# Two half transfers for every weight chunk, and a limit on those under way in the expert stage

## What is computed

```
x = even_layer(...)        # mixer (mLSTM + differential attention), then a SwiGLU of width 2816
x = odd_layer(...)         # convolution mixer, then moe_swiglu
x = hybrid_layer(...) x 2  # three kinds of attention, gate, layer norm

def moe_swiglu(u, router_w, w1, w3, w2):       # 8 experts of width 2816, top 2
    logits = (tokens @ router_w)
    top_vals, top_idx = lax.top_k(logits, TOP_K)
    gates = jax.nn.softmax(top_vals, axis=-1)
    ...
    return (jax.nn.silu(xb @ w1[e]) * (xb @ w3[e])) @ w2[e]     # each block of tokens with its expert's weights
```

## Time and profile before

| | us |
|---|---|
| timed runs, median (lowest to highest) | 2010.14 (2007.98 to 2010.35) |
| the profiled execution: its own time | 2011.3 |
| the profiled execution: span from first to last instruction | 2009.5 |
| TensorE busy in the span | 1806.1 (90%) |
| weight loads (PEld) / VectorE / ScalarE busy | 1474.0 / 825.6 / 391.2 |
| moved by DMA | 480.22 MB, 239 GB/s on the mean |
| granted TensorE clock, mean | 0.945 |

### The profile page before, as it was taken

How to read it: one execution, slowest core, us unless ns; L and a number is a source line. 1 busy time by engine, 2 the same in 40 slices (tenths; PEclk the granted TensorE clock), 3 DMA queues, 4 the chain that set the end, 5 groups by cost and what they waited for, 6 DMA issues and landing times. The chain is left out here.

```text
span 2009.5 us, 43104 instructions
## 1 busy us (share of the span) xinstructions
PE 1806.1 (90%) x18202; PEld 1474.0 (73%) x18202; DVE 825.6 (41%) x2248; ACT 391.2 (19%) x1107; POOL 2.3 (0%) x6
## 2 busy tenths in 40 slices
PE   6999897999989887999988989978969998899987
PEld 4686666888868765789687887777658876688766
DVE  3756562778958812111110101011123766227651
ACT  3332333000014232000000000000021233112331
POOL 0000000000000000000000000000000000000000
PEclk8999998999999886999999999999989988899988
DMA  9622332899973222999999999999983412234100
GB/s 391 242 106 89 121 143 88 313 359 354 382 287 126 98 112 106 398 417 345 388 419 390 326 368 354 421 418 370 377 367 126 168 64 84 84 126 168 43 1 21
DMA packets 67909, 480.22 MB, mean 239 GB/s; under 512 B 7424, under 2 KB 9728, under 8 KB 9856
## 3 DMA queue, kind: packets, MB, share of 16 engines
q1 hardware_dynamic: 67712, 477.39, 60.7%
HBM read 476.32 MB, written 1.05 MB: 238 GB/s over the span
## 5 line engine op out<-in xcount | busy, mean ns | idle before, releaser
L518 PE MATMUL PS<-sb_U,sb_ring 128*128 128x256 f32 (+1 forms) x1456 | 376.5, 417 | 16.3 <-PEq L249 9.9
L518 PEld LDWEIGHTS PS<-sb_U,sb_ring 128*128 128x128 f32 x1456 | 284.3, 198 | 96.1 <-issue 59.6
L1710 PE MATMUL PS<-sb_arena,sb_ring 128*64 128x98 f32 (+3 forms) x5632 | 221.8, 239 | 38.4 <-issue 36.3
L1710 PEld LDWEIGHTS PS<-sb_arena,sb_ring 128*64 128x64 f32 x5632 | 214.6, 139 | 46.5 <-issue 43.6
L1738 PE MATMUL PS<-sb_ring,sb_arena 128*64 128x256 f32 x1344 | 158.4, 384 | 4.8 <-issue 4.2
L518 PE MATMUL PS<-sb_arena 128*64 128x128 f32 (+9 forms) x884 | 153.7, 350 | 7.2 <-DVE sb_arena L751 4.4
L789 PE MATMUL PS<-sb_U,sb_ring 128*128 128x256 f32 x704 | 155.5, 383 | 4.7 <-PEq L249 4.7
L789 PEld LDWEIGHTS PS<-sb_U,sb_ring 128*128 128x128 f32 x704 | 134.8, 192 | 25.3 <-issue 7.4
L518 PEld LDWEIGHTS PS<-sb_arena 64*128 64x128 f32 (+4 forms) x884 | 108.9, 176 | 46.0 <-issue 25.7
L374 DVE SCALAR_TENSOR_TENSOR sb_arena<-sb_ring,sb_cs,sb_arena 128x256 f32<-128x256 f32 x280 | 135.8, 485 | 10.0
L1738 PEld LDWEIGHTS PS<-sb_ring,sb_arena 128*64 128x64 f32 x1344 | 98.3, 137 | 51.5 <-issue 7.1
(11 more groups left out here) (344 smaller groups left out, 1622.6 us busy)
## 6 DMA issues: line engine op xcount, KB each, us to landing
sb_ring<-stream SPq DMA_DIRECT2D x446, 1024.0 KB, 8.2
sb_arena<-stream SPq DMA_DIRECT2D x4, 1024.0 KB, 7.9
sb_consts<-consts SPq DMA_DIRECT2D x1, 1773.5 KB, 26.3
sb_U<-ctxT SPq DMA_DIRECT2D x1, 1024.0 KB, 7.5
sb_XT<-xT SPq DMA_DIRECT2D x1, 1024.0 KB, 9.3
out<-sb_XT SPq DMA_DIRECT2D x8, 128.0 KB, 2.0
sb_small<-small SPq DMA_DIRECT2D x1, 292.0 KB, 2.7
sb_consts<-consts SPq DMA_DIRECT2D x1, 129.0 KB, 2.7
```

Source lines behind the costliest of these rows:

```text
L518: ins = pe.transpose(o, l, r) if t.turn else pe.matmul(o, l, r, start=s, stop=e)
L1710: ins = pe.matmul(PS[c:c + 64, m % 4, h * T:h * T + n], w[:, h, kt, c:c + 64], src[:, kt, 0:n], start=(kt == 0), stop=(kt == KT - 1))
```

## The change

Each chunk is now moved by two DMAs, one for rows 0 to 63 and one for rows 64 to 127, each with a semaphore of its own (26 in place of 13). Whoever waits for a chunk waits for both. This holds in all stages. In the expert stage SP waits, before it issues a half, until the half that is three before it in the stream has landed; so at most three halves (one and a half chunks) are under way.

```
+UNDER_WAY = 3
...
-    def landing(self, g):
-        return self.landed[self.turn(g) % RING] if self.home(g) is None else self.home_landed[self.home(g)]
+    def landing(self, g, part):
+        n = RING + self.home(g) if self.home(g) is not None else self.turn(g) % RING
+        return self.landed[2 * n + part]
 
     def wait(self, eng, g):
-        eng.wait_ge(self.landing(g), 16 if self.home(g) is not None else 16 * (self.turn(g) // RING + 1))
+        for part in range(2):
+            self.wait_part(eng, g, part)
+
+    def wait_part(self, eng, g, part):
+
+        eng.wait_ge(self.landing(g, part), 16 if self.home(g) is not None else 16 * (self.turn(g) // RING + 1))
+
+    def send(self, sp, g, source, under_way=None):
+
+        for part in range(2):
+            if under_way is not None:
+                self.wait_part(sp, *divmod(2 * g + part - under_way, 2))
+            rows = slice(part * (P // 2), (part + 1) * (P // 2))
+            sp.dma_start(self.chunk(g)[rows, :], source[rows, :]).then_inc(self.landing(g, part), 16)
...
-            sp.dma_start(self.chunk(g), self.dram[self.base + g]).then_inc(self.landing(g), 16)
+            self.send(sp, g, self.dram[self.base + g])
...
                 for g in range(MOD_FIRST):
-                    sp.dma_start(ws.chunk(g), ws.dram[g]).then_inc(landed[g % RING], 16)
+                    ws.send(sp, g, ws.dram[g])
...
-                    sp.dma_start(ws.chunk(g), source).then_inc(ws.landing(g), 16)
+                    ws.send(sp, g, source, UNDER_WAY)
```

More of the change, by code:

```diff
@@ L167, with __init__ @@
 class Stream:
-    def __init__(self, nc, ring, dram, sems, homes, home_sems, home_first):
+    def __init__(self, nc, ring, dram, sems, homes, home_first):
         self.nc, self.ring, self.dram, self.landed = nc, ring, dram, sems
-        self.homes, self.home_landed, self.home_first = homes, home_sems, home_first
+        self.homes, self.home_first = homes, home_first
         self.used = self.issued = 0
@@ L228, in clear @@
     def clear(self):
-        clear_together(self.nc, self.landed + self.home_landed)
+        clear_together(self.nc, self.landed)
 class Stage:
@@ L342, in area @@
             return arena[:, at:at + n]
-        landed = [ctx.enter_context(nc.semaphore(f"landed{i}")) for i in range(RING)]
-        home_landed = [ctx.enter_context(nc.semaphore(f"home_landed{i}")) for i in range(len(HOMES))]
-        ws = Stream(nc, ring, a["stream"], landed, [area(at, CH) for at in HOMES], home_landed, PRE_CH - OUT_CH + RING)
+        landed = [ctx.enter_context(nc.semaphore(f"landed{i}")) for i in range(2 * (RING + len(HOMES)))]
+        ws = Stream(nc, ring, a["stream"], landed, [area(at, CH) for at in HOMES], PRE_CH - OUT_CH + RING)
         late = ctx.enter_context(nc.semaphore("late_inputs"))
```

## The result

The changed kernel takes 2658.35 us (median of 4 runs, 2653.46 to 2668.7) against 2010.24 for the kernel before: a ratio of 1.322, 95% interval 1.319 to 1.326. The prediction was 2029 with a range of 1983 to 2075. The sign was right, but by luck: the two terms that gave it make 19 us of the 648 us measured, a factor of 34, and the cause named was the wrong one.

The account below looks back on a forecast made before the run. The prediction took the expert stage's weight DMA as the bound, with TensorE's instruction stops behind its shortfall; 11 us of stream plus 8 us of barrier on 2011.3, less 1.2, gave 2029 us, range 1983 to 2075.

Parts of the forecast that it names:

- the two terms that gave it: Expert stage: weight stream 11 us longer and 8 us more at the barrier, together 19 us.
- Halves in all stages: All stages: extra issues and waits taken as 0, range to 13 us; halves themselves 0, at most 0.33 us a chunk.
- the ports rival: Weight transfers: each half reaches only half of the SBUF's ports, a chunk takes 4.98 us, total about 2800 us; chance 0.10.
- The limit's stream term: Expert stage: under the limit the weight stream takes 727 us in place of 716.5, 11 us longer.
- The window just covers the latency: Expert stage: a half's turn takes 3.65 to 3.7 us, three halves fill the engines for 3.74 us, no slack.
- window too short: Expert stage: a turn takes 3.9 to 4 us and all packets cost 1.07 us, 46 us more, 2075; chance 0.07.
- 80 us for the instruction packets: Expert stage: 75 of 94 instruction packets each cost the weight stream 1.07 us, 80 us in all.
- The stops for instructions: TensorE, expert stage: 52.1 us of waits for its own instructions; fewer transfers under way should remove 40 us.
- The barrier: End of the expert stage: SP issues the last half late and all engines wait for it, 8 us more.
- Second wait and second issue: Per chunk, one more issue of 0.33 us on SP and one more TensorE wait: taken as 0, range to 13 us.
- a DMA packet time that doubles (ports): DMA queue: a doubled packet time was named as a sign of the forecast being wrong, pointing to half the SBUF's ports.
- the signs of being right: Expert stage: short instruction stops, weight waits of 40 us and more, DMA share under 0.95, SP late, stream some 727 us.

Follow-up runs that it names:

- the probe: A kernel that computes nothing, only copies x and moves twelve chunks per cut; whole chunks took 2.49 us each, the change's halves 2.41 us each.
- even_rows_limit4: The changed kernel with halves cut by even and odd rows and at most four halves under way in the expert stage: 2079.18 us, ratio 1.036.
- whole_limit2: The kernel before with whole chunks and at most two under way in the expert stage: 2068.79 us, ratio 1.027.
- even_rows_limit3: The changed kernel with halves cut by even and odd rows, still at most three halves under way: 2231.99 us, ratio 1.109.

## Why the prediction was wrong

**The step that failed** is the one under "Halves in all stages": "I take 0, the same bytes going in the same 8 KB rows." It measures 542 us with no limit (27% of the time): a chunk of two such halves takes 4.82 us in the probe (twice 2.41), and not 2.49. The upper end that the step allowed, 0.33 us a chunk, was too low as well. The rows of before could not show it, since all their transfers span 128 rows; that was said, and yet I took the value at one end. The reason given, same bytes and same packets, does not bear on it: a packet's length says nothing of how many ports its transfer spreads over. I gave the ports rival 0.10. It deserved most of the chance, because the page of the Trainium skill that was named with it (SBUF — State Buffer, Door 1: The DMA port swizzle) gives a measured rate for partitions 0 to 63, 196 GB/s, and no row spoke against it.

**The ports rival's own sum**, "about 2800", was too long by 140 us. It took a chunk at 4.98 us; 4.82 in the probe is a little less. The expert stage grew by 513 us (578 forecast), the dense one by 114 (154) and the head by 19 (60): I priced all 81 chunks of a window of 250 us and all of the first 60 us; the stages themselves are 244 and 43 us long, and by the rows above the dense stage took in 78 MB (218 GB/s x 358.6 us) and not 85. The word "serialize" that the prediction quotes beside this rival stands in the next section of the Trainium skill's page (SBUF — State Buffer, "Can I just issue two DMAs to hit both halves?"); the probe agrees for one queue, with 60.1 us for the halves in turn and 32.6 and 32.7 for each alone.

**The limit's stream term**, "11 us longer", was mis-sized as well. The turn was worked out as 3.65 to 3.7 us against 3 x 1.25 = 3.74. With the ports right a half lands 5.0 us after its issue on the median, so three under way move at most 3 x 0.524 MB / 5.0 us = 315 GB/s (284 to 306 in the slices) and not 421. The limit of three halves costs 2232.0 - 2014.7 = 217 us there, and 102 us with the change's rows, where a turn is longer but the ports are the bound already. By columns the same sum gives 3 x 0.524 / 5.6 = 281 GB/s (262 to 280 in the slices). "The window just covers the latency" took the 2.3 us measured on an idle queue for a queue that is not idle. A half needed 3.6 us at the least, 5.0 on the median with two before it, and 5.8 with three before it (even_rows_limit4). Which part of the way grows, the runs don't tell. So the rival "window too short", which I gave 0.07 and 46 us, had the right mechanism at a fifth of its size. The other part of the term, 80 us for the instruction packets, no run measured by itself.

**The stops for instructions**: "I take 40 us" is about what limit 2 gives (47.9 to 11.1 in two lines), but only with two chunks under way. The reading of the earlier trace rows, that two or three chunks give shorter stops than five or six, is borne out for two; three and four leave them at 36 to 39 us at L1712. That the stops are waits for instructions rests on the rows that the prediction reads (254 instructions from one to the next); no run tried it. In the changed kernel the row cannot be read for it, as waits for weights also go under "issue".

**The barrier**: right in kind. Forecast 8 us; 9 with whole_limit2, of which the stage gave back 5.7 and the time about 10 without the limit on the last nine; SyncE 23 us late in the changed kernel, three times the forecast, as its halves land at half the rate. In even_rows_limit3 it is 16 us late (1716.2 against 1699.7), a part of the 217 us.

**Second wait and second issue**: forecast 0 (range to 13); measured 0, with an interval of about -2 to +10 us.

**What would have shown it**: the sign named, "a DMA packet time that doubles (ports)", is the one that came, 330 to 584 ns (1.8 times on the mean), and "other stages that differ by more than 2 us" with it. Of the signs of being right, the waits for weights and for SyncE came too, for the other reason; a DMA share under 0.95 did not (0.99).

## What to carry to other kernels

Cut a transfer by columns or by every second row, never at row 64: the halves 0 to 63 and 64 to 127 run at about half the rate (218 GB/s on one queue, 242 on two), and a stage that takes weights faster than that pays for it. A limit on transfers under way is sized by bytes over the landing time with the queue filled; here three chunks of 1 MB cost nothing that can be seen, two cost 3% and three halves 11% (cut by even and odd rows). Where no row of a trace has the shape that a change brings in, a measured price from elsewhere for that very shape weighs more than the argument that bytes and packets stay the same.

## What the runs showed of the hardware that I had not expected

- A stretch of 64 contiguous rows runs at full rate if it lies across row 64 (rows 32 to 95: 422 GB/s), and four quarters of 32 rows in turn run at half (217 GB/s).
- The DMA share does not show a port bound: 0.99 at 223 GB/s. Only the GB/s row beside it does.
- With no limit the change's halves reach 254 to 290 GB/s in some slices, more than they did in the probe (218 on one queue, 242 on two).
- TensorE's stops at "issue" change with the weight transfers that are queued: 8.5 us at L1712 with two chunks under way, 36.3 with three; with four halves, the same bytes as two chunks, 27.1.
